# The RMSNorm ahead of w_up and the final RMSNorm of a hybrid decoder layer, done by column blocks, with the transposes between the first chunks of w_up

## What is computed

```python
def rmsnorm(x, g):
    x32 = x.astype(jnp.float32)
    y = x32 * lax.rsqrt(jnp.mean(x32 * x32, axis=-1, keepdims=True) + EPS)
    return (y * g.astype(jnp.float32)).astype(x.dtype)

    x = x + y.astype(x.dtype) @ w_out              # (256, 2048)
    xn = rmsnorm(x, norm_ffn_g)
    hid = causal_dwconv(xn @ w_up, ffn_conv_w)     # w_up: 2048 x 11264
    u, gt = hid[..., :D_FF], hid[..., D_FF:]
    x = x + (jax.nn.silu(gt) * u) @ w_down
...
    return rmsnorm(x, norm_final_g)
```

## Time and profile before

| | us |
|---|---|
| time, median of 3 runs | 1839.68 (1837.96 to 1841.13) |
| span of the profiled execution | 1838.6 |
| w_out's last matmul to w_up's first | 10.68 |
| first chunk of w_up | 3.40 |
| second chunk of w_up (nothing waits in it) | 2.79 |
| last matmul of w_down to the end of the span | 9.58 |

### The profile page before, as it was taken

The page is one execution under the profiler, slowest core; times in us unless marked ns, Lnnn a source line. Parts: engine busy times, 40 slices in busy tenths (PEclk is TensorE's granted clock), DMA queues, the critical chain, the costliest instruction groups (busy, mean ns, idle before and its releaser), DMA issues.

```text
span 1838.6 us, 28288 instructions
## 1 busy us (share of the span) xinstructions
PE 1817.3 (99%) x10949; PEld 1567.1 (85%) x10949; DVE 1065.3 (58%) x1279; ACT 826.7 (45%) x910; POOL 434.0 (24%) x242
## 2 busy tenths in 40 slices
PE   8999999999999999999999999999999999999997
PEld 6888898888888888888888878888888888888886
DVE  5678736366555755555556366666666666633334
ACT  5555333436433544444444354444444444444444
POOL 5222431121221222222222232222222222222223
PEclk9999999999999999999999999999999999999999
DMA  6666544444554566666667646666666666665663
GB/s 199 178 180 180 148 116 135 130 138 139 165 154 121 155 207 182 197 192 184 188 188 244 202 148 185 183 190 190 189 184 190 188 191 184 213 195 186 196 194 134
DMA packets 263436, 324.58 MB, mean 177 GB/s; under 512 B 16779, under 2 KB 230213, under 8 KB 262725
## 3 DMA queue, kind: packets, MB, share of 16 engines
q1 hardware_dynamic: 263366, 323.58, 58.2%
HBM read 321.45 MB, written 2.10 MB: 176 GB/s over the span
## 4 chain that ended last, share of the span: by engine, by line
PE 97%; DVE 1%; ACT 1%; DMA 0%; issue 0%; DVEq 0%; SPq 0%; ACTq 0%
PE ps L578 96%; PE ps L659 0%; DVE xs L1808 0%; DMA x_in<-in_x_dram 0%; PE ps L690 0%; PE ps L872 0%; PE ps L849 0%; ACT w_hi L376 0%; ACT p L994 0%; DVE x L1791 0%; ACT junk L994 0%; ACT x_sq L994 0%; PE ps L955 0%; DVE fmax L1448 0%; DVE p L1443 0%
## 5 line engine op out<-in xcount | busy, mean ns | idle before, releaser
L376 ACT ACTIVATE w_hi<-raw 128x1024 fp32r<-128x1024 f32 x601 | 635.1, 1059 | 877.5 <-PE ps L578 866.4
L381 DVE TENSOR_TENSOR w_lo<-raw,w_hi 128x1024 fp32r<-128x1024 f32 x450 | 561.5, 1254 | 490.7 <-ACT w_hi L376 489.8
L578 PE MATMUL ps<-xnT,w_hi 128*128 128x512 f32 (+1 forms) x2960 | 748.7, 394 | 0.7 <-issue 0.7
L381 POOL TENSOR_TENSOR w_lo<-raw,w_hi 128x1024 fp32r<-128x1024 f32 x151 | 366.7, 2428 | 1305.6 <-ACT w_hi L376 1305.6
L578 PEld LDWEIGHTS ps<-xnT,w_hi 128*128 128x128 f32 (+1 forms) x2960 | 532.4, 189 | 99.4 <-issue 1.5
L578 PEld LDWEIGHTS ps<-xnT,w_lo 128*128 128x128 f32 (+1 forms) x2960 | 403.9, 190 | 29.0
L578 PE MATMUL ps<-xnT,w_lo 128*128 128x256 f32 (+1 forms) x2960 | 415.2, 282 | 0.0
L578 PE MATMUL ps<-w_hi,xnT 128*128 128x512 f32 x1408 | 356.4, 392 | 0.0
L578 PEld LDWEIGHTS ps<-w_hi,xnT 128*128 128x128 f32 x1408 | 261.8, 188 | 54.7 <-issue 0.7
L578 PE MATMUL ps<-w_lo,xnT 128*128 128x512 f32 x704 | 192.2, 389 | 0.0
L578 PEld LDWEIGHTS ps<-w_lo,xnT 128*128 128x128 f32 x704 | 132.1, 188 | 27.8 <-DVE w_lo L381 0.2
(11 more groups left out here) (325 smaller groups left out, 1031.0 us busy)
## 6 DMA issues: line engine op xcount, KB each, us to landing
raw<-in_w_in_dram SPq DMA_DIRECT2D x256, 512.0 KB, 3.8
raw<-in_w_up_dram SPq DMA_DIRECT2D x176, 512.0 KB, 3.9
raw<-in_w_down_dram SPq DMA_DIRECT2D x88, 512.0 KB, 4.4
raw<-in_w_out_dram SPq DMA_DIRECT2D x32, 512.0 KB, 4.5
raw<-in_w_fox_proj_dram SPq DMA_DIRECT2D x16, 512.0 KB, 4.2
raw<-in_w_gdn_proj_dram SPq DMA_DIRECT2D x16, 512.0 KB, 4.3
raw<-in_w_ml_proj_dram SPq DMA_DIRECT2D x16, 512.0 KB, 4.0
x_in<-in_x_dram SPq DMA_DIRECT2D x4, 512.0 KB, 6.0
```

The lines of the kernel that those rows point to most:

```text
L376: act.activation(w_hi[:, s, 0:n], raw[:, s, 0:n], ACT.Copy).then_inc(hi_ready[s], 1)
L381: eng.tensor_tensor(w_lo[:, s, 0:n], raw[:, s, 0:n], w_hi[:, s, 0:n], ALU.subtract).then_inc(lo_ready[s], 1)
L578: return pe.matmul(o, l, r, start=start, stop=stop)
```

## The change

`last_rows` ends the columns 1024 to 1535 of tile 1 ahead of columns 1536 to 2047. The residual of tile 1 is added in three pieces instead of two (`PIECES`). Tile 0 is multiplied by the weight before the root is known and scaled by the root later, in place; the second half of it is weighted by GpSimd and scaled by ScalarE. GpSimd starts on a signal of VectorE (`xg_ready`) and does no scaling. The chunks N3 to N3+3 of w_up are all split by VectorE. The transposes are issued by 512-column block: TensorE turns block j of both tiles directly ahead of chunk j, with four banks used in turn. In the final norm the store is five DMAs instead of three.

```diff
+        PIECES = ((0, 0, 1024), (0, 1024, D), (1, 0, 1024), (1, 1024, 1536), (1, 1536, D))
...
-        TURNS = ((0, 0), (0, 1), (1, 0), (1, 1), (0, 2), (1, 2), (0, 3), (1, 3))
+        TURNS = tuple((tt, n) for n in range(4) for tt in range(NT))
...
+        def turn_bank(tt, n):
+
+            return 4 + 2 * (n % 2) + tt
...
+            for tt, a, b, done, n in ((0, 0, 1024, "xs_ready", 11), (0, 1024, D, "xs_act", 2), (1, 0, 1024, "xs_ready", 12),
+                                      (1, 1024, 1536, "xs_act", 3), (1, 1536, D, "xs_ready", 13)):
+                sp.wait_ge(S[done], n)
+                sp.dma_start(of[:, tt, a:b], xs[:, tt, a:b]).then_inc(S["stored"], 16)
+            sp.wait_ge(S["stored"], 16 * 5)
...
+                for q in range(2):
+                    for k2 in range(2):
+                        s = (c0 + 2 * k2 + 1) % SLOTS
+                        last = three(ps[:, 6 + q, :], x2[:, k2, :], 1, s, 512 * q, 512 * q + 512, False, k2 == 1)
+                        if q == 1:
+                            last.then_inc(chunk_used[s], 1)
+                    if q == 0:
+                        last.then_inc(S["block_done"], 1)
...
+            def turn_rows_again(tt, n):
+
+                pe.wait_ge(S["x1_ready"], 3 if n == 0 else 5)
+                if n >= 2:
+                    pe.wait_ge(S["xt_ready"], 2 * (n - 2) + tt + 1)
+                if tt == 0 and n >= 2:
+                    pe.wait_ge(S["xs_act"], 1)
+                else:
+                    pe.wait_ge(S["xs_ready"], {(0, 0): 5, (0, 1): 7, (1, 0): 6, (1, 1): 8, (1, 2): 9, (1, 3): 10}[tt, n])
+                for t in range(4):
+                    kt = 4 * n + t
+                    last = pe.transpose(ps[:, turn_bank(tt, n), t * P:t * P + P], xs[:, tt, kt * P:kt * P + P], ident[:, :])
+                last.then_inc(S["xt_written"], 1)
+
+            def up_round(i, first=False):
                 for v in range(2):
                     pe.wait_ge(up_read[v], i + 1)
                     for j in range(8):
-                        if v == 0 and j < 4:
-                            pe.wait_ge(S["xt_ready"], (3, 4, 6, 8)[j])
+                        if first and v == 0 and j < 4:
+                            for tt in range(NT):
+                                turn_rows_again(tt, j)
+                            pe.wait_ge(S["xt_ready"], 2 * j + 2)
                         columns(N3 + 8 * v + j, i * 4, xnT, 4 * (j % 4), KT, 4 * v + 2 * (j // 4))
...
+            def scale_late(p):
+
+                act.wait_ge(S["rstd_ready"], 2 * p + 1)
+                act.wait_ge(S["xs_pool"], p + 1)
+                f(xs[:, 0, 1024:D], xs[:, 0, 1024:D], ACT.Identity, scale=rstd[:, 1, 2 * p:2 * p + 1], bias=0.0).then_inc(S["xs_act"], 1)
+
+            def norm_second(p):
+
+                total = square(p, 2)
+                chain(f(norm_b[:, p, 1:2], total, ACT.Identity, scale=1.0 / D, bias=eps_c[:, 0:1]))
+                if p:
+                    scale_late(p)
+                total = square(p, 3)
+                chain(f(norm_c[:, p:p + 1], total, ACT.Identity, scale=1.0 / D, bias=norm_b[:, p, 1:2]))
+                total = square(p, 4)
+                f(rstd[:, 1, 2 * p + 1:2 * p + 2], total, ACT.Sqrt, scale=1.0 / D, bias=norm_c[:, p:p + 1]).then_inc(S["sums_ready"], 1)
...
+            norm_first(0)
+            split_hi(act, N3)
+            norm_second(0)
+            for k, (tt, n) in enumerate(TURNS):
+                act.wait_ge(S["xt_written"], 4 + k + 1)
+                dst, src = turned(tt, n)
                 f(dst, src, ACT.Copy).then_inc(S["xt_hi"], 1)
+                if k == 0:
+                    scale_late(0)
+                elif tt == 1 and n < 3:
+                    split_hi(act, N3 + n + 1)
...
+            norm_start(0, N3 - 4)
+            scale(0, 0, 0, 512)
+            add_piece(0, N3 - 4, 4)
+            split_lo(dve, N3)
+            root(0, 1)
+            weigh_and_scale(0, 1, 0, 512)
+            turn_lo(0, 0)
+            scale(0, 0, 512, 1024)
+            turn_lo(1, 0)
+            for n in range(1, 4):
+                weigh_and_scale(0, 1, 512 * n, 512 * n + 512)
+                turn_lo(0, n)
+                split_lo(dve, N3 + n)
+                turn_lo(1, n)
...
+            norm_start(1, N5 - 4)
+            scale(1, 0, 0, 1024)
+            dve.wait_ge(S["xs_ready"], 11)
+            dve.sem_inc(S["xg_ready"], 1)
+            add_piece(1, N5 - 4, 4)
+            weigh(1, 1, 0, 1024, 3)
+            root(1, 1)
+            scale(1, 1, 0, 1024)
+            weigh_and_scale(1, 1, 1536, D)
...
+            weigh(0, 0, 1024, D, 2, 1)
             rounds(N3, FF // 512, 16)
             rounds(N4, FKT // 2 - 1, 4)
             pool.wait_ge(S["gfin_loaded"], 16)
+            weigh(1, 0, 1024, D, 2, 2)
+            weigh(1, 1, 1024, 1536, 4, 3)
```

More of the change, by code:

```diff
@@ L1233, in _, with square @@
             mixed_hi(3)
-            def norm_rows(p, after):
-                f(spare[:, :], eps_c[:, :], ACT.Sqrt)
[L1238 to L1249, removed]
+            def square(p, k):
+                tt, a, b = PIECES[k]
+                total = ss[:, 1, 4 * p + k:4 * p + k + 1] if k < 4 else ss[:, 0, 4 + p:5 + p]
+                act.wait_ge(S["x1_ready"], 5 * p + k + 1)
+                chain(f(junk[:, 0:b - a], x1[:, tt, a:b], ACT.Square, accum_out=total))
+                return total
@@ new lines, in norm_first @@
+            def norm_first(p):
+                f(spare[:, :], eps_c[:, :], ACT.Sqrt)
+                total = square(p, 0)
+                chain(f(norm_b[:, p, 0:1], total, ACT.Identity, scale=1.0 / D, bias=eps_c[:, 0:1]))
+                total = square(p, 1)
+                f(rstd[:, 1, 2 * p:2 * p + 1], total, ACT.Sqrt, scale=1.0 / D, bias=norm_b[:, p, 0:1]).then_inc(S["sums_ready"], 1)
+            def scale_late(p):
+                act.wait_ge(S["rstd_ready"], 2 * p + 1)
+                act.wait_ge(S["xs_pool"], p + 1)
+                f(xs[:, 0, 1024:D], xs[:, 0, 1024:D], ACT.Identity, scale=rstd[:, 1, 2 * p:2 * p + 1], bias=0.0).then_inc(S["xs_act"], 1)
@@ L1287, in _ @@
                           ACT.Copy).then_inc(S["side_hi"], 1)
-            norm_rows(1, lambda: None)
+            norm_first(1)
+            norm_second(1)
+            act.wait_ge(S["rstd_ready"], 4)
+            act.wait_ge(S["xs_pool"], 3)
+            f(xs[:, 1, 1024:1536], xs[:, 1, 1024:1536], ACT.Identity, scale=rstd[:, 1, 3:4], bias=0.0).then_inc(S["xs_act"], 1)
         @block.vector
@@ new lines, in weigh, with scale, weigh_and_scale @@
+            def weigh(p, tt, a, b, k):
+                dve.wait_ge(S["x1_ready"], 5 * p + k)
+                chain(tt_(xs[:, tt, a:b], x1[:, tt, a:b], (gfin if p else gffn)[:, a:b], ALU.mult))
+            def scale(p, tt, a, b):
+                dve.wait_ge(S["rstd_ready"], 2 * p + tt + 1)
+                return dve.tensor_scalar(xs[:, tt, a:b], xs[:, tt, a:b], rstd[:, 1, 2 * p + tt:2 * p + tt + 1], None,
+                                         ALU.mult).then_inc(S["xs_ready"], 1)
+            def weigh_and_scale(p, tt, a, b):
+                dve.wait_ge(S["rstd_ready"], 2 * p + tt + 1)
+                dve.scalar_tensor_tensor(xs[:, tt, a:b], x1[:, tt, a:b], rstd[:, 1, 2 * p + tt:2 * p + tt + 1],
+                                         (gfin if p else gffn)[:, a:b], ALU.mult, ALU.mult).then_inc(S["xs_ready"], 1)
@@ new lines, in turn_lo, with norm_start @@
+            def turn_lo(tt, n):
+                dve.wait_ge(S["xt_hi"], 4 + 2 * n + tt + 1)
+                dst, src = turned(tt, n, SEQ)
+                tt_(dst, src, turned(tt, n)[0], ALU.subtract).then_inc(S["xt_ready"], 1)
+            def norm_start(p, c0):
+                add_piece(p, c0, 0)
+                add_piece(p, c0, 1)
+                weigh(p, 0, 0, 1024, 1)
+                dve.sem_inc(S["xg_ready"], 1)
+                add_piece(p, c0, 2)
+                root(p, 0)
+                add_piece(p, c0, 3)
@@ L2018, in _ @@
             pool.wait_ge(S["gfin_loaded"], 16)
-            for tt in range(NT):
-                scale_tile(1, tt)
+            weigh(1, 0, 1024, D, 2, 2)
+            weigh(1, 1, 1024, 1536, 4, 3)
 _INS = ['x', 'norm_mix_g', 'w_in', 'fox_f_bias', 'gdn_conv_w', 'gdn_a_log', 'gdn_dt_bias', 'gdn_norm_g',
```

118 lines of the change are left out of this document (36 added, 82 removed).

## The result

The changed kernel takes 1845.2 us in the median (1845.02 to 1851.13 over five runs) against 1839.68 for the kernel before (now five runs as well, 1837.96 to 1841.13). The ratio of the two is 1.0037, with a 95% interval of 1.0026 to 1.0048: slower, by 6.8 us (4.8 to 8.8). The two medians lie only 5.5 us apart; executions of one kernel differ by more than that, so the ratio with its interval says more. The forecast was 1846.7 us, 7.0 more than before.

What follows compares the result with a forecast made beforehand. TensorE, busy 1817.3 of 1838.6 us, was taken as the bound. A loss of 8.2 us ahead of chunk N3+4 less 1.2 gained at the end gave +7.0 on 1839.68, 1846.7 us; low 1842.5, high 1854.

Steps and rivals of the forecast that it cites:

- The first block: Between the last matmul of w_out and chunk N3: the wait falls from 10.68 to 5.43 us, a gain of 5.25.
- Three gaps: Ahead of chunks N3+1 to N3+3: TensorE waits 3.81 us each for transposes, copy, subtractions and weight split, 11.43 in all.
- short gaps: Rival: the weight split is off the waiting line, gaps of 2.67 us ahead of later chunks, 1841.7 us; chance 0.15.
- faster: Rival: only the eight transposes stand between chunks, gaps below 1.1 us on average, 1835.3 us; chance 0.08.
- The clock: Chunks N3 to N3+3 run partly at 1.2 GHz: 1.1 us for the first, 0.5 for each other, 2.6 together.
- the sign that the prediction gave for its forecast: Granted TensorE clock from 1085 to 1115 us in the changed trace: 0.9 or more.
- cold chunks: Rival: chunks N3 to N3+3 each start and mostly run at 1.2 GHz, costing 9.3 us instead of 2.6, 1853.4 us; chance 0.22.
- Middle: From w_out's last matmul to chunk N3+4: a loss of 5.57 us plus 2.6 for the lower clock, 8.2 together.
- The end: Behind the last matmul of w_down: later root but shorter weighting and smaller last store, a gain of 1.2 us.
- That GpSimd would hold up the weighting of tile 1: In the final norm: if GpSimd's last piece delayed it until the root, up to 0.7 us of the gain would go.
- The sum: Whole kernel: 8.2 us lost less 1.2 gained, +7.0, median 1846.7 us; chance 0.55 for 1844 to 1850.5.

Runs made afterwards that it cites:

- the filler run: Changed kernel plus three float32 filler matmuls on TensorE ahead of chunk N3, two behind the first four transposes, one behind the next four; ratio 1.0043 to the kernel before.
- the long filler: Changed kernel plus seven float32 filler matmuls on TensorE ahead of chunk N3, five behind the first four transposes, two behind the next four; ratio 1.0044 to the kernel before.

## Why the prediction was right, step by step

- **The first block.** Forecast 5.43 us, measured 5.38. ScalarE's squares, the reciprocal, one piece at 0.74, four transposes, copy and subtraction came as summed, within 0.1 each. ScalarE's second copy waits for the transposes ahead of it and not for `scale_late`, as had been forecast.
- **Three gaps.** Forecast 3.81 each (the terms listed add up to 3.80), measured 3.75, 3.74 and 3.74, and the split in them 1.14 forecast, 1.15 by its removal. This step decided the sign: 11.2 us of new waits against 5.3 won ahead of chunk N3. The rivals "short gaps" and "faster" supposed that copy, split and subtraction overlap; the order of the programs did not allow it. With the transposes one chunk ahead, there were no gaps at all.
- **The clock.** Forecast 1.1 for chunk N3 and 0.5 for each of the others, 2.6; in the profile 1.68 and three times 0.11, 2.0. The sum was near by luck, as chunk N3 was priced too low and the others too high. Over the 29.8 us the clock averages 0.94, which is the sign that the prediction gave for its forecast. The 0.11 is there at a clock of 1.00 as well, so it is the start behind a wait and not the clock. Over executions the term is not one number: the filler run had 2.5 and 1.7 in the two chunks behind. The price of the lower level was read from a row, eight matmuls in 3.75 us, for whose stretch the trace gives a granted clock of 1.00, so that row shows no level by itself; the filler run bears the price out, with eight in 3.78 us at 0.50. The "cold chunks" rival did not happen in full anywhere. The rule of the Trainium skill that was quoted for it ("TensorE: Matmul & The Clock Gate", section "HAM oscillation — how this bites in real kernels"), that every batch behind a wait starts at the lower level, does not carry over to these gaps: three chunks behind gaps of 3.75 us, of which TensorE waited 2.71, ran at 1.00. The section describes a kernel with longer waits, so it is not refuted either.
- **Middle.** Forecast a loss of 8.2, measured 7.33.
- **The end.** Forecast a gain of 1.2, measured 0.55 between the two profiles; this is the term that was mis-sized. How far is not settled: against the other profile of the old end, that of the kernel with GpSimd silent (10.46), the same end gains 1.4. The root came 0.43 later (forecast 0.4) and the last issue 0.75 earlier (0.9). The 0.3 us taken for the smaller last store did not show: the way from its issue to the end of the span got longer by 0.2 against the profile before (shorter by 0.7 against the other). Among the changed ends it is longest, 4.3, when stores follow each other closely. `scale` of 1024 columns took 0.75 us without GpSimd beside it (forecast 0.9). By the Trainium skill's rule that the prediction quoted ("VectorE: DVE Perf Modes", section "Mode 2×_2P") it was estimated at 0.7, so that rule agrees here. That GpSimd would hold up the weighting of tile 1 happened, 1.80 us instead of 1.22, but it was over 0.66 us before the reciprocal started, so it cost nothing.
- **The sum.** +7.0 forecast, +6.8 by stages and by the ratio, 5.5 between the medians. Part of the closeness is luck: the loss in the middle came out 0.9 smaller and the gain at the end 0.65 smaller, and the two errors cancel. The mechanism, three gaps made by the round trip through ScalarE and VectorE, is what the experiments bear out.

What the change brings for itself is worth having: with GpSimd silent VectorE's pieces take 0.74 us. It was spent, and more, on putting transposes between chunks without anything else for TensorE to do.

## What to carry to other kernels

When work is moved in between two stages that ran back to back, count the whole way through every engine that it crosses, not its own length: eight transposes of 0.9 us cost 3.75 each time, because their results went through two other engines before TensorE could go on. Issue such work at least one batch ahead of its use, and look in the other engines' programs for an instruction that has time, standing ahead of one that has none. Before reordering anything, look whether an engine is slow because of a neighbour: here one engine's silence alone was worth 2.8 us (ratio 0.9985).

## What was not expected of the hardware

- TensorE's clock in short gaps is not settled by the gap. Behind 3.74 us with 1.04 us of transposes in it, a chunk ran at 1.00 in two profiles of the changed kernel and at 0.50 in the run with the short filler. More work shortly before does not explain it, as behind the long filler the same chunk ran in 2.90 us.
- In the kernel with the transposes ahead of chunk N3 the clock fell at about 1090, behind two waits; 20 transposes back to back took 4.01 us, most of it at 0.50. The clock rose again at about 1093.5, ahead of the first matmul of chunk N3 (1093.86), with nothing but transposes on TensorE since 1090.1.
- A float32 matmul of 512 columns (identity times a float32 tile) shows as two records of 0.43 us each.
- The way from the last store's issue to the end of the span is not fixed. With the same stores issued at the same places it was 3.64 us in one profile and 4.52 in another; with the changed ends it was 3.6 with four stores, 3.8 to 3.9 with five, and 4.3 when the last ones follow each other closely.
